# A tile's lead copy opens more projection segments in a two-layer hybrid trunk

## The reference

```
for layer in range(2):
    g = norm_gains[layer]
    h = rmsnorm(x, g[0])
    m = mixer_ab(h, ...) if layer % 2 == 0 else mixer_cd(h, ...)
    x = x + rmsnorm(m, g[1])
    x = x + rmsnorm(cross_attn(rmsnorm(x, g[2]), mem, ...), g[3])
    x = x + rmsnorm(sq_relu_mlp(rmsnorm(x, g[4]), ...), g[5])
```

## Time and profile before

| | |
|---|---|
| median of 3 runs | 890.69 us |
| lowest, highest | 889.92, 890.82 us |
| profiled execution, its own time | 890.24 us |
| its span, first to last instruction | 888.5 us |
| TensorE busy | 870.8 us |
| VectorE busy | 625.2 us |
| ScalarE busy | 479.0 us |
| GpSimd busy | 156.9 us |

### The profile page before, as it was taken

One profiled execution on the slowest core, in us unless ns is written; L12 is line 12 of the kernel. 1 busy time (PEld: TensorE's weight loads), 2 busy tenths in 40 slices (PEclk: granted clock), 3 DMA queues, 4 the chain that ended last, 5 costly groups with the idle time before them and its releaser, 6 DMA issues.

```text
span 888.5 us, 14750 instructions
## 1 busy us (share of the span) xinstructions
PE 870.8 (98%) x6078; PEld 798.3 (90%) x6078; DVE 625.2 (70%) x971; ACT 479.0 (54%) x699; POOL 156.9 (18%) x155
## 2 busy tenths in 40 slices
PE   8999999999999999999999999999999899999997
PEld 8999988898899999999899989888998799999996
DVE  5886996786487655555579999976686575555554
ACT  6864655665475444444664443447675565444443
POOL 1210900000000000000028888660000000000000
PEclk9999999999999999999999999999999999999999
DMA  8654435544455556655566675445543456555551
GB/s 288 188 165 146 140 125 181 170 141 144 161 177 187 192 193 199 195 192 191 177 179 191 184 224 160 151 165 173 178 148 112 145 181 210 197 196 192 190 193 69
DMA packets 82954, 155.27 MB, mean 175 GB/s; under 512 B 6838, under 2 KB 8776, under 8 KB 82888
## 3 DMA queue, kind: packets, MB, share of 16 engines
q1 hardware_dynamic: 82776, 154.29, 53.7%
q10 hardware_dynamic: 112, 0.05, 0.0%
HBM read 152.11 MB, written 1.05 MB: 172 GB/s over the span
## 4 chain that ended last, share of the span: by engine, by line
PE 79%; DVE 14%; DMA 2%; ACT 2%; POOL 1%; issue 1%; DVEq 0%; POOLq 0%; SPq 0%; ACTq 0%
PE ps L561 14%; PE ps L563 13%; PE ps L562 13%; PE ps L629 10%; PE ps L630 10%; PE ps L631 10%; DVE ps L1914 4%; DVE w_lo L1555 3%; DMA raw<-in_ab_w_in 2%; DVE cv L2096 2%; DVE xT L1836 1%; PE ps L687 1%; DVE h_lo L1566 1%; PE ps L937 1%; PE ps L938 1%
## 5 line engine op out<-in xcount | busy, mean ns | idle before, releaser
L1129 ACT ACTIVATE w_hi<-raw 128x1024 fp32r<-128x1024 f32 x284 | 295.7, 1055 | 211.5 <-DMA raw<-in_mlp_w 124.5
L1555 DVE TENSOR_TENSOR w_lo<-raw,w_hi 128x1024 fp32r<-128x1024 f32 x246 | 296.1, 1225 | 114.8 <-ACT w_hi L1129 114.3
L561 PE MATMUL ps<-h_hi,w_hi 128*128 128x256 f32 x1108 | 310.8, 281 | 5.9 <-POOL w_lo L2220 3.8
L563 PE MATMUL ps<-h_hi,w_lo 128*128 128x256 f32 x1108 | 308.4, 278 | 0.0
L562 PE MATMUL ps<-h_lo,w_hi 128*128 128x256 f32 x1108 | 308.4, 278 | 0.0
L561 PEld LDWEIGHTS ps<-h_hi,w_hi 128*128 128x128 f32 x1108 | 209.5, 189 | 8.7 <-POOL w_lo L2220 4.5
L562 PEld LDWEIGHTS ps<-h_lo,w_hi 128*128 128x128 f32 x1108 | 209.4, 189 | 0.1
L563 PEld LDWEIGHTS ps<-h_hi,w_lo 128*128 128x128 f32 x1108 | 208.9, 189 | 0.0
L2249 POOL TENSOR_TENSOR rfac<-stat,mhalf 128x1 f32<-128x1 f32 (+2 forms) x18 | 16.7, 926 | 640.3 <-DVE stat L1810 522.1
L629 PE MATMUL ps<-w_hi,r_hi 128*128 128x512 f32 x256 | 99.8, 390 | 0.0
L630 PE MATMUL ps<-w_lo,r_hi 128*128 128x512 f32 x256 | 99.7, 389 | 0.0
(11 more groups left out here) (282 smaller groups left out, 1250.3 us busy)
## 6 DMA issues: line engine op xcount, KB each, us to landing
raw<-in_mlp_w SPq DMA_DIRECT2D x128, 512.0 KB, 3.7
raw<-in_cd_w_in SPq DMA_DIRECT2D x40, 512.0 KB, 4.0
raw<-in_xa_wkv SPq DMA_DIRECT2D x32, 512.0 KB, 3.7
raw<-in_ab_w_in SPq DMA_DIRECT2D x24, 512.0 KB, 4.7
raw<-in_xa_wq SPq DMA_DIRECT2D x16, 512.0 KB, 3.7
raw<-in_xa_wo SPq DMA_DIRECT2D x16, 512.0 KB, 3.7
raw<-in_cd_w_out SPq DMA_DIRECT2D x16, 512.0 KB, 3.5
raw<-in_ab_w_out SPq DMA_DIRECT2D x12, 512.0 KB, 3.4
```

What stands on the lines that cost most here:

```text
L561: nc.tensor.matmul(dst, wt[0], x[0], start=start, stop=False, skip_group_check=True)
L563: return nc.tensor.matmul(dst, wt[1], x[0], start=False, stop=stop, skip_group_check=True)
L1129: nc.scalar.activation(w_hi[:, v % SLOTS, :, :], raw[:, v % SLOTS, :, :], ACT.Copy)\
L1555: V.tensor_tensor(w_lo[:, v % SLOTS, :, :], raw[:, v % SLOTS, :, :], f(w_hi[:, v % SLOTS, :, :]), ALU.subtract).then_inc(lo_ready_dve, 1)
```

## The change

One more pair of lead operations is made in each layer's input stage, and more segments open with the copy: in layer 0 ("xbc", 2), ("z", 0) and ("z", 1); in layer 1 the eight segments from the third on; in both MLPs w1(1) as well. TensorE waits for lead_lo before ("xbc", 2), before the third segment of layer 1 and, one segment earlier than before, at w1(1).

```diff
+        lead = (lead_hi[:, :], lead_lo[:, :])
...
-            project(("xbc", 2), [("xbc", 2, 0), ("xbc", 2, 1)], h_src)
-            project(("z", 0), [("z", 0, 0), ("z", 0, 1)], h_src)
+            pe.wait_ge(dve_made, after("dve", "lead", "in0"))
+            project(("xbc", 2), [("xbc", 2, 0), ("xbc", 2, 1)], h_src, lead=lead)
+            project(("z", 0), [("z", 0, 0), ("z", 0, 1)], h_src, lead=lead)
...
-            project(("z", 1), [("z", 1, 0), ("z", 1, 1)], h_src)
+            project(("z", 1), [("z", 1, 0), ("z", 1, 1)], h_src, lead=lead)
...
-                            project(name, dest, h_src, ready=h_ready("in1") if n == 0 else None, tail=2 if n else 0)
+                            if n == 2:
+                                pe.wait_ge(dve_made, after("dve", "lead", "in1"))
+                            project(name, dest, h_src, ready=h_ready("in1") if n == 0 else None, tail=2 if n else 0,
+                                    lead=lead if n >= 2 else None)
...
-                    if h == 2:
+                    if h == 1:
                         pe.wait_ge(dve_made, after("dve", "lead", l))
...
-                            lead=(lead_hi[:, :], lead_lo[:, :]) if h >= 2 else None)
+                            lead=lead if h else None)
...
             round_to(F_[("xbc", 1)] + 4)
+            nc.scalar.activation(lead_hi[:, :], xT[:, 0, :], ACT.Identity, scale=gain(0, 0, 0))\
+                .then_inc(act_made, tick("act", "lead", "in0"))
...
                     round_to(F_[("a", 0)] + 5)
+                    nc.scalar.activation(lead_hi[:, :], xT[:, 0, :], ACT.Identity, scale=gain(1, 0, 0))\
+                        .then_inc(act_made, tick("act", "lead", "in1"))
...
             for i in range(2, 4):
                 scaled_u(i)
+            dve.wait_ge(act_made, after("act", "lead", "in0"))
+            V.scalar_tensor_tensor(out=lead_lo[:, :], in0=xT[:, 0, :], scalar=gain(0, 0, 0), in1=f(lead_hi[:, :]),
+                                   op0=ALU.mult, op1=ALU.subtract).then_inc(dve_made, tick("dve", "lead", "in0"))
...
                     low_to(F_[("a", 0)] + 3)
+                    dve.wait_ge(act_made, after("act", "lead", "in1"))
+                    V.scalar_tensor_tensor(out=lead_lo[:, :], in0=xT[:, 0, :], scalar=gain(1, 0, 0), in1=f(lead_hi[:, :]),
+                                           op0=ALU.mult, op1=ALU.subtract).then_inc(dve_made, tick("dve", "lead", "in1"))
```

## The result

The changed kernel takes 893.22 us (median of 8 runs, 892.13 to 894.47), the kernel before on the same chip 890.76 us (8 runs, 889.92 to 891.26): a ratio of 1.0029, 95% interval 1.0018 to 1.0040. It is 2.5 us slower, 1.6 to 3.6 by the interval. 893.8 was forecast. The profiled execution of the changed kernel is its quickest, 892.13 us, with a span of 890.4 us against the 888.5 of the earlier trace rows.

The account below looks back on a forecast made before the run. TensorE, busy 98% of the span, was taken to bound the kernel. Wait less stall +2.44, clock +1.5, pace -0.6 gave +3.3 us: 893.5 on the profile's scale, 894.0 on the median's, 893.8 said; range 891.0 to 895.4.

Parts of the forecast that it names:

- The wait: Before ("xbc", 2) in layer 0: TensorE waits 2.8 us for lead_lo, less a 0.36 us stall, net +2.44 us.
- The clock: Behind the new wait at ("xbc", 2): TensorE's granted clock falls to half, +1.5 us, given 7 in 10.
- Rival (a): At ("xbc", 2): same wait without a fall of the clock, that segment possibly quick too; +1.6 us, 892.3; chance 0.25.
- The pace in layer 0: Lead quickens ("z", 0), ("z", 1) and w1(0, 1) by half of 0.4 us each, ("xbc", 2) by nothing; -0.6 us.
- sign of the forecast: Whole kernel: slower, meaning over 892.5 us, given 0.74; same 0.22, faster 0.04.
- Layer 1: Layer 1's input projection: lead operations fit idle time and are free, segment pace taken 0; bounds -0.3 and +0.7 us.
- Rival (c): Layer 0: lead_lo ready before ("xbc", 2), so no wait, and pace gained in all four segments; -1.6 us, 889.1; chance 0.03.
- Rival (b): Lead gives no pace behind transposes and h segments; +3.9 us, 894.6, or 895.3 if layer 1 turns slow; chance 0.2.
- rule of two independent ports: TensorE reads moving operand and weights through separate ports, so the copy's address could not matter and pace would be 0.
- Rival (d): Layer 1's input projection: quick pace or a shifted wait removes its own clock fall, -1.5 us; sum +1.8, 892.5; chance 0.05.

Follow-up runs that it names:

- e1: Changed kernel with VectorE's layer 0 lead_lo made before the dt values instead of behind scaled_u(3); 891.40 us, ratio 1.0010 to the kernel before.
- e2: Kernel before plus only layer 0's lead operations and TensorE's wait before ("xbc", 2), matmuls still reading h; 892.98 us, ratio 1.0025 to before.
- e6: e1 with lead_hi and lead_lo placed 448 instead of 768 bytes behind a multiple of 1,024, as h; 894.62 us, ratio 1.0049 to before.
- e7: e1 with layer 1's input stage as in the kernel before; 890.56 us, ratio 1.0000 to before.
- e5: Changed kernel with 24 unused identity products on TensorE before its wait at ("xbc", 2); 895.91 us, ratio 1.0063 to before.
- e8: Changed kernel with 12 unused identity products on TensorE before its wait at ("xbc", 2); 891.97 us, ratio 1.0014 to before.
- a2: The changed kernel run and profiled a second time, no edit; 892.29 us.
- b1: The kernel before, run and profiled a second time, no edit; 889.66 us.
- b2: The kernel before, run and profiled a third time, no edit; 890.20 us.
- e3: Kernel before with only w1(1) of both layers opening with lead; 890.73 us, ratio 1.0003 to before.
- e4: Kernel before with only layer 1's lead operations, wait and eight input segments on lead; 890.77 us, ratio 1.0002 to before.

## Why the prediction was right, and where it was off

**The wait.** Forecast: ("xbc", 2) opens 2.8 us later, at 39.4 to 39.6, with an idle of 2.6 to 2.8 us put down to lead_lo, and the stall half way goes. It opened at 39.61, 2.79 later when the 0.16 from upstream is taken off; the idle was 2.55, the matmul after it starting late by itself; the stall of the earlier trace rows is gone. e1, where only lead_lo's place differs, takes the wait and most of the loss away, and e2, where only the wait is left, has the loss. This step is shown.

**The clock.** Forecast: a fall with 7 in 10, worth 1.5 us. It came in two of four executions with that gap, and in none of those where the gap was missing (e1, e6, e7) or filled (e5, e8). Its size can be read from the same segment at the same pace: 12.63 us in the profile after, 11.00 in e2, so 1.63 us. The timed runs fit it and don't prove it: e8 is 1.1 us nearer to its before than the changed kernel is to its own (uncertain by 1.3), and the mean clocks of the changed kernel and the one before differ by 0.9 us (uncertain by 1.1), where 0.5 to 0.7 falls of 1.63 us are 0.8 to 1.1. So the size of the term was right, and its chance, as far as four executions tell, somewhat high. Rival (a) is what a2 and e2 are at this place.

**The pace in layer 0.** Forecast: nothing in ("xbc", 2), half of 0.4 us in each of ("z", 0), ("z", 1) and w1(0, 1), so -0.6. In the profile after all three had the full 0.4 (-0.41, -0.39, -0.39), and ("xbc", 2), quick on both sides of the fall of its clock, another 0.39. The account up to 87.52 then closes: 2.79 - 0.36 - 0.39 + 1.63 - 0.41 - 0.39 = +2.87, and the table has 3.03 - 0.16 = 2.87. This was the term that was mis-sized, by 1.0 us with w1(0, 1) counted. The question behind it, does lead make the pace, had two halves. Yes: outside e6, 235 of the 249 segments that opened with lead were at the quick pace after six matmuls, two more fell to half clock so early that it can't be told, and e6 shows that the address does it. In the MLPs not one was slow. And no: the twelve slow ones are ("xbc", 2) in e1, e7, a2 and e5, ("z", 0) and ("z", 1) in e5, and six in layer 1, and without lead ("z", 0) and ("z", 1) were quick in b1, b2, e2 and e3. Lead makes the quick pace likelier, not certain, and least so at ("xbc", 2), as the prediction feared.

The plainest test is a segment that follows another with no break between them; each execution has seven, ("z", 0) and six in layer 1. Opened with h, all 42 went on at the pace of the segment before them, 20 quick and 22 slow. Opened with lead, without e6, 37 stayed quick, and of the 12 that were entered at the slow pace six turned quick. In e6, with lead at h's alignment, the two that were entered slow stayed slow. a2 shows a change at ("z", 0), with 24 matmuls from the first row to the second and from the third to the fourth:

```profile
48.25 0.28 PE L563 MATMUL ps<-h_hi,w_hi 128*128 128x256 f32 x1
...
51.08 0.28 PE L563 MATMUL ps<-lead_hi,w_hi 128*128 128x256 f32 x1
...
52.24 0.28 PE L564 MATMUL ps<-h_lo,w_hi 128*128 128x256 f32 x1
...
54.96 0.28 PE L564 MATMUL ps<-h_lo,w_hi 128*128 128x256 f32 x1
```

So an h segment takes over the pace that it is entered with, and lead can break the slow one.

**Why that pace brought nothing in e1, e3 and e7.** The prediction said that it would be wrong if a stage after 75 us had slack that the waits don't show. What the waits of before didn't show was VectorE's cbm: an execution that comes early to 77.9 us waits for it. The changed kernel comes 3 us late, so there the gain of ("z", 0) and ("z", 1) counts in full and only makes the loss smaller. The other reason is the yardstick. ("z", 0) and ("z", 1) were quick in two of the three profiles of the kernel before, w1(0, 1) in one, so against its usual execution lead wins less than the 0.4 us apiece of the earlier trace rows. For w1(0, 1), the one segment that e3 could quicken, it is the only reason of the two, as it lies far behind cbm; and 0.4 us is less than e3's runs can tell. The sign of the forecast was safe all the same: a wait of 2.44 us net is more than all the pace that could be won, 1.6.

**Layer 1.** Forecast: VectorE's lead_lo goes into 1.36 us of idle time, free; the rest 0. The step failed. The idle time was there, but GpSimd's low half was running beside it, and lead_lo was done at 466.01, where the prediction had it done before 463. In each of the eight executions with lead_lo at that place it took 2.60 to 2.61 us and ended 0.28 us after GpSimd's, against 0.47 to 0.48 at its other places; Rsq, started under the same GpSimd instruction, was held in the same way in each of the six others (1.16 or 1.17 us against 0.41). The Trainium skill states this, on the page "SBUF — State Buffer", section "Who interferes with whom": a VectorE instruction with two inputs in SBUF contends with a GpSimd instruction that reads SBUF, because the second input comes through a shared port, and the page calls such contention an exclusive lock. The trace agrees: 2.61 instead of 0.47 us. The net price is 0.34 us on the chain of VectorE and GpSimd. Over the whole projection, from 467.78 to 562.84, the six executions without layer 1's part gain 0.44 us on the profile before (0 to 0.69), and the eight with it lose 0.19 (from 0.57 gained to 0.78 lost): a difference of 0.6. Falls of the clock have a part in it: five of the eight have one in this stretch, and two of the six. Among the executions without a fall there the difference is 0.2 (0.36 gained against 0.59). The timed runs say 0.9 (e1 against e7) and 0.2 (e4 against before, by the ratios), with uncertainties of 1.5 and 1.2 us, so they don't show this price by themselves; their mean clocks differ the same way, by 0.8 and 0.6 us. The prediction's bounds, -0.3 to +0.7, held it; its reason "free" did not. How the price is shared is open: it was not tried to place lead_lo elsewhere, and the quicker segments may lengthen the waits for GpSimd, with a fall behind them. Those waits are 3.2 to 5.4 us, on average 4.3, in the eight executions and 2.7 to 4.1, on average 3.6, in the six.

**Rival (c)**, that the wait doesn't arise, was built as e1, and is no faster than before: -1.6 us was its price, +1.0 came (interval -0.2 to +2.0). Without layer 1's part (e7) it was 0.0, so the 1.6 us of pace was not there to be had, for the two reasons above. **Rival (b)**, no pace at all, falls with e6 and the account above. The Trainium skill's rule of two independent ports, which the prediction set beside it ("TensorE: Matmul & The Clock Gate", "Step-by-step: what each phase is for"), says nothing of an address, and as the prediction read it, it has no room for the 10.91 and 11.31 us that the same matmuls took with the copy at two addresses; here the measurement decides. **Rival (d)**, that layer 1 loses its fall of the clock, rested on a fall that is no fixture: of three executions of the kernel before, one has a fall in layer 1's projection, and of three of the changed kernel two. In a2 there is none, but one of twice the length at 703.6.

**The sum by stages.** Three executions of the changed kernel against three of the one before, mean shifts from the table: +2.78 us up to 87.52 (forecast 3.5), -0.77 from there to 467.78 (forecast -0.2; w1(0, 1), and the pace of h segments, which happened to be quick more often), +0.55 in layer 1's projection (forecast 0), -0.08 from there to the end. Together 2.48, and the medians differ by 2.46. So the forecast of +3.3 on its own scale was 0.8 too high: the pace, with what fell to the h segments, was too small by some 1.0, the clock at 1.5 where two falls in three make 1.1 (0.4 too high), and layer 1 was missing its 0.55 the other way. That these misses partly cancel is luck; the wait, the largest term, was right for its own reason.

**Open** is what sets the pace of a segment that opens with h behind a break, why the clock falls behind one gap and not behind its twin, and why an address 320 bytes off does what it does.

## What to carry to other kernels

Before an engine is made to wait for something new, look where the producer stands in its own program and not how short it is: a copy of 0.5 us cost 2.5 us of wait because it stood behind work that ended 2 us after TensorE was ready, and in two of four executions another 1.6 us of clock. Idle time on VectorE was not free for an instruction with two inputs in SBUF while GpSimd ran one that reads SBUF. And a gain of 0.4 us per segment that one profile shows may be an execution's own luck: profile the same kernel twice before building on it.

## What the runs showed of the hardware

- The same 96 float32r matmuls of 256 columns go 113.4 or 117.9 ns apart, and within a segment they keep their pace, in all but one case, as long as no wait and no fall of the clock comes between; behind either it can change. A segment that followed another without a break kept that one's pace in 42 cases of 42. Three matmuls that read the moving operand from another address (768 instead of 448 bytes behind a multiple of 1,024) turned it quick in six of 12 such segments that were entered slow, and in all 156 segments w1(l, 2) to w1(l, 7) outside e6, where with the other address all twelve were slow. Over the executions of one kernel the slow segments change.
- A VectorE instruction of 0.47 us was held to 2.61 us by a GpSimd instruction of 2.85 us that had started 0.52 us earlier. It ended 0.28 us behind it, and this in eight executions of eight.
- Behind the same 2.5 us gap TensorE's granted clock fell to half for 3.3 us in two of four executions. Behind the wait for mt, at about 700 us, it fell in all five executions in which that wait was 1.6 or 1.7 us, and in two of the nine in which it was 1.3 to 1.5.
- A float32 product of 128 columns is two matmuls in the trace, 0.11 us each.
